# Later places for the prompt-attention and gated-attention pieces among the stretches of the cached attention

## The chip, the cores and the metric

The kernel runs on one core of one Trainium2 chip. The metric is the device time of one execution in microseconds (us). Engines are named as in the profile: PE (TensorE matmul), PEld (its weight load), DVE (VectorE), ACT (ScalarE), POOL (GpSimd) and SP (SyncE, which issues nearly all transfers here).

## What is computed

One decoder layer runs for a prompt group (256 rows) and a sample group (8 sequences of 8 new rows). Between two feed-forward sublayers stands the mixer, whose two head groups share one projection:

```python
qm, km, vm, qg, kg, vg, gg, log_a = mixer_projections(h, pos, w_mix_in, w_gk_up, b_gk)
o_moba = moba_fn(qm, km, vm)          # prompt: causal softmax; sample: top-3 of 8 cached blocks + own rows
o_gla, s_fin = gla_chunked(qg, kg, vg, log_a, gla_s0, gla_chunk)
o_gla = gla_output(o_gla, gg, gla_norm_g, x.dtype)
mix = jnp.concatenate([o_moba, o_gla], axis=-1) @ w_mix_out
x = post_norm_residual(x, mix, m[:, 5], 1.0, ln_g[1], ln_b[1])
```

For the samples `moba_fn` reads a paged cache of 2048 past keys and values per sequence, 8 heads of 64 (`cache_k`, `cache_v`, 256 pages of 256 KB in all). For the prompt it is a plain causal attention over 256 rows. `gla_chunked` is the gated linear attention with a carried state per head.

## The kernel before

The program is written out by hand, engine by engine: each engine has its own list of steps in program order, and semaphores order the lists against each other. The change lies in the stage after the mixer's projections, from about 420 to 630 us of the profile, in which three things are woven together.

**The cached attention.** The 8 sequences go in 4 pairs, i = 0 to 3. A pair's 16 pages of keys per sequence come in four stretches j = 0 to 3 (512 keys of each sequence). A stretch is: PE turns 8 key pages (`turn_keys`, L1046, four 128x128 transposes a page into one PSUM bank); ACT and DVE copy each bank into `kT` (L1445 and L2090, shared between them by `on_act`); PE multiplies with the queries (`scores`, L1057); DVE takes the block sums and block maxima from the scores (`block_values`, L2097 and L2099), and only then ACT copies the scores into `prob` (`scores_out`). After a pair's fourth stretch comes its opening of the softmax: DVE picks the blocks (`choose`, ten small steps L2117 to L2128), ACT takes nine exponentials (`exps`), PE turns the probabilities (`turn_probs`, L1077 and L1079, five banks), DVE copies banks 0, 1 and 4 and ACT banks 2 and 3 into `PT` (`probs_dve`, L2146; `probs_act`), and PE multiplies with the value pages (`values`, L1095) group by group. `own_heads` (DVE L2154), `pick_heads` (PE L1110), `out_high` (ACT) and `out_low` (DVE L2160) carry the result of a pair out. The stretches of pair i+1 run between the value groups of pair i.

**The transfers.** A group is 4 pages, 1 MB. SP issues the 64 groups in the order of `PAGE_GROUPS`; each waits until the group that last held its buffer has been used. There are four ring buffers and one in `pages_h`/`pages_l`; a sixth (`IN_M`, inside the projections `M`) and a seventh (`IN_W`, inside `W`) join later, at the groups that `BEGIN_AT` names, once the projections and the turned prompt values that lie there are no longer needed.

**The pieces.** The prompt's attention and the gated attention are cut into pieces k = 0 to 19 (`mix(k)`, one function on PE, ACT and DVE each). Pieces 0 to 6 are the prompt's attention, two heads at a time and pipelined: scores on PE (L1119, L1120), mask and maximum on DVE (`prompt_max`, L2169 to L2174), exponentials on ACT, normalising on DVE (`prompt_norm`, L2179 to L2182), transposes on PE (L1126), copies on ACT, values on PE (L1135 to L1137), rounding on ACT and DVE (L2186). Pieces 12 to 19 are the gated attention's output and states: 13 and 14 the outputs (L1173 to L1181), 16 a logarithm and an exponential on ACT over 128x1280, 16 to 19 the sample states (PE L1218, DVE L2270 and L2261, two sequences a piece), 17 the scaled output on DVE (L2317), 18 its high half on ACT, 19 its low half on DVE (L2320). Nothing is left in pieces 7 to 11 here: they ran during the projections.

`point(x)` is a place in the weave; `AT_POINT` maps it to a piece. Place 0 to 2 lie in the stretches j = 1 to 3 of pair 0; for pair i the places from 4i+3 on are: 4i+3 first after the scores of its fourth stretch, 4i+4 after the value groups of the second sequence of pair i-1, 4i+5 and 4i+6 in the first two stretches j that follow. (For pair 0, place 3 lies in the first and 4 in the second stretch of pair 1, 5 and 6 in the third and fourth.)

**PSUM.** Every turned page, score, probability or piece takes one of five banks in rotation. PE may fill a bank once ACT or DVE has copied out what was filled five places earlier (`turn_bank`), so a late copy of either engine stops PE.

After the last key stretch PE also starts the output projection: `early_slot(0)` (L836 to L841) waits for `go_done`, the end of piece 19 on DVE; `early_slot(1)` follows among the last value groups.

Of the kernel before, what the change touches and what calls it, by code (L numbers as in the profile page):

```python
# [183 lines left out]
GAPS[10] += [("nvg", t) for t in range(3)]  # L184
FILLS = [key for gap in GAPS for key in gap]
IN_MI = len(FILLS)
AT_POINT = {0: 0, 1: 1, 2: 2} | {x: x - 1 for x in range(4, 8)} | {x: x + 4 for x in range(8, 14)} | {15: 18, 16: 19}


def point_fills(x):  # L190
# [6 lines left out]
for _i in range(NPAIR):  # L197
    _m = 4 * _i + 3
    if _i == 0:
        PAGE_GROUPS += [("k", 1, j, bi) for j in range(2) for bi in range(2)]  # L200
        PAGE_GROUPS += [("v", 0, 0, 0)] + [("k", 1, 2, bi) for bi in range(2)] + [("v", 0, 1, 0)]
        PAGE_GROUPS += [("k", 1, 3, bi) for bi in range(2)] + [("v", 0, 2, 0), ("v", 0, 3, 0)]
        FILLS += key_fills(1, 0) + point_fills(_m) + key_fills(1, 1) + point_fills(_m + 1)
        FILLS += [("p", 0, q) for q in range(5)] + key_fills(1, 2) + point_fills(_m + 2) + [("own", 1)]
        FILLS += key_fills(1, 3) + point_fills(_m + 3)
        continue
    FILLS += point_fills(_m) + point_fills(_m + 1)
    if _i:
        PAGE_GROUPS += [("v", _i - 1, g, 1) for g in range(4)]
        FILLS += [("pick", _i - 1)]  # L210
    FILLS += [("p", _i, q) for q in range(5)]
    for _j in range(4):
        if _i + 1 < NPAIR:
            PAGE_GROUPS += [("k", _i + 1, _j, bi) for bi in range(2)]
            FILLS += ([("own", _i + 1)] if _j == 3 else []) + key_fills(_i + 1, _j)
            FILLS += point_fills(_m + 2 + _j) if _j < 2 else []
        PAGE_GROUPS += [("v", _i, _j, 0)]
PAGE_GROUPS += [("v", NPAIR - 1, g, 1) for g in range(4)]
FILLS += [("pick", NPAIR - 1)]
GROUP_AT = {key: n for n, key in enumerate(PAGE_GROUPS)}  # L220
FILL_AT = {key: n for n, key in enumerate(FILLS)}
IN_RING, IN_H, IN_M, IN_W = range(GROUPS), GROUPS, GROUPS + 1, GROUPS + 2
BEGIN_AT = {GROUP_AT[("v", 1, 1, 0)]: IN_M, GROUP_AT[("v", 2, 0, 0)]: IN_W}
LAST_IN = {IN_H: GROUP_AT[("v", 2, 3, 0)], IN_M: GROUP_AT[("k", 3, 3, 1)], IN_W: GROUP_AT[("v", 3, 0, 0)]}


# [123 lines left out]
def layer_kernel(nc, a, o):  # L350
    ctx = ExitStack()
    with ctx:
# [250 lines left out]
        def _(sp):  # L603
# [73 lines left out]
            def load_pages(n):  # L677

                kind, i, g, bi = PAGE_GROUPS[n]
                cache = a["cache_k"] if kind == "k" else a["cache_v"]  # L680
                _, page = nc.values_load_multi_w_load_instructions(
                    pages[0:1, bass.ds((2 * i + bi) * NPAGE + 4 * g, 4)], engines=[mybir.EngineType.SP],
                    min_val=0, max_val=NPHYS - 1,
                    skip_runtime_bounds_check_because="a page table holds numbers of physical pages")
                b = BUF[n]
                if GROUP_BEFORE[n] is not None:
                    wait_used(GROUP_BEFORE[n])
                elif b == IN_H:
                    sp.wait_ge(used, MI + 12)
                elif b == IN_M:  # L690
                    sp.wait_ge(tp_filled, FILL_AT[("po", 3)] + 1)
                elif b == IN_W:
                    sp.wait_ge(stored, 4 * 16)
                    sp.wait_ge(tp_filled, FILL_AT[("go", 3)] + 1)
                else:
                    sp.wait_ge(lo_ready, split_through(MI + 8 + (b - RING_AT[MI]) % R))
                for j in range(4):
                    sp.dma_start(page_at(b, j), cache[bass.ds(page[j], 1), :, :].rearrange("o s f -> s (o f)")
                                 ).then_inc(page_landed[b], 16)
# [67 lines left out]
        def _(pe):  # L767
# [570 lines left out]
            for i in range(NPAIR):  # L1338
                m0 = 4 * i + 3
                if i == 0:  # L1340
                    turn_keys(1, 0, 0)
                    turn_keys(1, 0, 1)
                    point(m0)
                    scores(1, 0)
                    turn_keys(1, 1, 0)
                    turn_keys(1, 1, 1)
                    point(m0 + 1)
                    scores(1, 1)
                    turn_probs(0)
                    values(0, 0, 0)  # L1350
                    turn_keys(1, 2, 0)
                    turn_keys(1, 2, 1)
                    values(0, 0, 1)
                    point(m0 + 2)
                    scores(1, 2)
                    own_scores(1)
                    turn_keys(1, 3, 0)
                    turn_keys(1, 3, 1)
                    values(0, 0, 2)
                    values(0, 0, 3)  # L1360
                    point(m0 + 3)
                    scores(1, 3)
                    continue
# [8 lines left out]
                for j in range(4):  # L1372
                    if i + 1 < NPAIR:
                        if j == 3:
                            own_scores(i + 1)
                        turn_keys(i + 1, j, 0)
                        turn_keys(i + 1, j, 1)
                    if i == NPAIR - 1 and j == EARLY_SLOT[0]:
                        pe.wait_ge(go_done, 1)
                        wait_dve(("po", HP - 1))  # L1380
                        early_slot(0)
                    values(i, 0, j)
                    if i + 1 < NPAIR:
                        if j < 2:
                            point(m0 + 2 + j)
                        scores(i + 1, j)
            for g in range(4):
                if g == EARLY_SLOT[1]:
# [52 lines left out]
        def _(act):  # L1441
# [296 lines left out]
            for i in range(NPAIR):  # L1738
                m0 = 4 * i + 3
                if i == 0:  # L1740
# [4 lines left out]
                    keys_act(1, 1, 0)  # L1745
                    keys_act(1, 1, 1)
                    exps(0, 6, 9)
                    point(m0 + 1)
                    probs_act(0)
                    scores_out(1, 0)  # L1750
                    scores_out(1, 1)
                    keys_act(1, 2, 0)
                    keys_act(1, 2, 1)
                    point(m0 + 2)
# [12 lines left out]
                if i + 1 < NPAIR:  # L1767
                    for j in range(4):
                        keys_act(i + 1, j, 0)
                        keys_act(i + 1, j, 1)  # L1770
                        if j < 2:
                            point(m0 + 2 + j)
                        scores_out(i + 1, j)
            act.wait_ge(s_out, 8 * NPAIR)
            high(At(MO))
            high(At(MO + 1))
# [36 lines left out]
        def _(dve):  # L1813
# [591 lines left out]
            for i in range(NPAIR):  # L2405
                m0 = 4 * i + 3
                block_values(i, 3)
                if i == 0:
                    keys_dve(1, 0, 0)
                    keys_dve(1, 0, 1)  # L2410
                    choose(0)
                    point(m0)
                    keys_dve(1, 1, 0)
                    keys_dve(1, 1, 1)
                    block_values(1, 0)
                    point(m0 + 1)
                    block_values(1, 1)
                    probs_dve(0, 0)
                    probs_dve(0, 1)
                    totals(0)  # L2420
                    probs_dve(0, 4)
                    keys_dve(1, 2, 0)
                    keys_dve(1, 2, 1)
                    point(m0 + 2)
# [17 lines left out]
                if i + 1 < NPAIR:  # L2442
                    for j in range(4):
# [5 lines left out]
                            point(m0 + 2 + j)  # L2449
                        if j < 3:  # L2450
                            block_values(i + 1, j)
            low(At(MO))
            low(At(MO + 1))
            own_heads(NPAIR - 1)
            out_low(NPAIR - 1)
# [176 lines left out]
```

## Time and profile before

| | us |
|---|---|
| median of 3 runs | 912.74 |
| lowest and highest | 911.48, 916.84 |
| the profiled execution, own time | 915.75 |
| its span, first to last instruction | 914.0 |
| PE busy | 861.1 (94%) |
| DVE busy | 552.1 (60%) |
| ACT busy | 349.0 (38%) |
| HBM read | 196.04 MB |

PE is busy nearly all the time; the stage of the cached attention is where it is not: there its idle time is 22.33 us of 205 (425 to 630 us). A busy PE is also not a PE at full clock: the profile lists the granted clock by slices, and in this stage it falls below 1.00 in several.

### The profile page before, as it was taken

To read this page: it belongs to the slowest core of one execution; us is meant where nothing else is said; L and a number is where in the kernel's file an instruction comes from. 1 tells how busy PE (TensorE), PEld (TensorE's weight loads), DVE (VectorE), ACT (ScalarE), POOL (GpSimd) and SP (SyncE) were. 2 spreads that over 40 slices of the span, in tenths; PEclk is the share of its full clock that TensorE was granted. 3 is DMA by queue.
4 is the path that set the end of the run, shared out by engine and by line. 5 is a ranking of instruction groups with operands and counts; after the bars stand their busy time and mean duration, and the time that the engine had idled before them with its cause. 6 is when DMAs were issued, how large, how long until landed. Compare 5 with 4: busy or idle time off the path is not lost. (4 is left out here: it accounts for less than half of the span.)

```text
span 914.0 us, 17041 instructions
## 1 busy us (share of the span) xinstructions
PE 861.1 (94%) x6857; PEld 758.8 (83%) x6857; DVE 552.1 (60%) x873; ACT 349.0 (38%) x494; POOL 27.8 (3%) x32
## 2 busy tenths in 40 slices
PE   5899999999999999999888998989999999999994
PEld 2588888889999599997566876678799999999993
DVE  1545445545665798785775466662886765555556
ACT  2423222323433654544655335441343322333331
POOL 0000000000000000000000000000300000000002
PEclk9999999999999999999999899999999999999997
DMA  9999898888756544456869989997836555534521
GB/s 318 349 287 276 245 271 254 249 240 226 236 147 216 184 140 151 155 166 218 292 191 362 386 308 386 346 377 239 228 86 171 159 139 143 144 103 128 159 64 57
DMA packets 209028, 200.96 MB, mean 220 GB/s; under 512 B 9601, under 2 KB 161293, under 8 KB 208822
## 3 DMA queue, kind: packets, MB, share of 16 engines
q1 hardware_dynamic: 207556, 196.04, 68.8%
q0 software_dynamic: 704, 2.49, 0.7%
q10 hardware_dynamic: 690, 1.35, 0.5%
q8 instruction: 54, 0.88, 0.4%
q14 instruction: 24, 0.20, 0.1%
HBM read 196.04 MB, written 3.80 MB: 219 GB/s over the span
## 5 line engine op out<-in xcount | busy, mean ns | idle before, releaser
L1826 DVE TENSOR_TENSOR wl<-raw,wh 128x2048 fp32r<-128x2048 f32 x90 | 206.7, 2298 | 90.5 <-ACT wh L1445 90.1
L780 PE MATMUL B<-Hh,wh 128*128 128x320 f32 x864 | 258.9, 313 | 0.4 <-ACT wh L1445 0.3
L781 PE MATMUL B<-Hl,wh 128*128 128x320 f32 x864 | 255.0, 309 | 0.0
L1445 ACT ACTIVATE wh<-raw 128x2048 fp32r<-128x2048 f32 x90 | 172.2, 1913 | 139.4 <-PE B L785 93.3
L780 PEld LDWEIGHTS B<-Hh,wh 128*128 128x128 f32 x864 | 162.1, 188 | 17.3 <-issue 16.2
L781 PEld LDWEIGHTS B<-Hl,wh 128*128 128x128 f32 x864 | 162.3, 188 | 0.3
L785 PE MATMUL B<-Hh,wl 128*128 128x320 f32 x864 | 144.2, 309 | 0.0
L785 PEld LDWEIGHTS B<-Hh,wl 128*128 128x128 f32 x864 | 131.1, 188 | 0.0
L780 PE MATMUL B<-Gh,wh 128*128 128x320 f32 x352 | 104.4, 311 | 0.0
L781 PE MATMUL B<-Gl,wh 128*128 128x320 f32 x352 | 103.8, 309 | 0.0
L1445 ACT ACTIVATE sg<-B 128x320 f32<-128x320 f32 x46 | 20.1, 437 | 194.0 <-PE B L785 179.7
L2007 DVE TENSOR_TENSOR hf<-sg,B 128x320 f32<-128x320 f32 x44 | 21.4, 487 | 100.3 <-ACT sg L1445 100.3
L780 PEld LDWEIGHTS B<-Gh,wh 128*128 128x128 f32 x352 | 66.1, 188 | 0.8 <-issue 0.8
L781 PEld LDWEIGHTS B<-Gl,wh 128*128 128x128 f32 x352 | 66.1, 188 | 0.0
L785 PE MATMUL B<-Gh,wl 128*128 128x320 f32 x352 | 56.8, 309 | 0.0
L1046 PE MATMUL B<-cst,ring 128*128 128x128 f32 x368 | 48.5, 286 | 6.4 <-ACT kT L1445 3.4
L1046 PEld LDWEIGHTS B<-cst,ring 128*128 128x128 f32 x368 | 42.3, 146 | 14.2 <-issue 6.7
L785 PEld LDWEIGHTS B<-Gh,wl 128*128 128x128 f32 x352 | 52.9, 188 | 0.0
L2090 DVE COPY kT<-B 128x512 f32<-128x512 f32 x62 | 41.2, 686 | 16.2 <-PE B L1046 16.1
L1445 ACT ACTIVATE kT<-B 128x512 f32<-128x512 f32 x66 | 36.0, 606 | 13.5 <-PE B L1046 13.5
L882 PE MATMUL B<-raw,cpk 128*32 128x512 f32 x272 | 37.4, 634 | 2.8 <-DMA raw<-in_w_ada 2.5
L1095 PE MATMUL B<-ring,PT 128*32 128x128 f32 x800 | 26.2, 280 | 8.7 <-DMA ring<-in_cache_v 4.6
(286 smaller groups left out, 935.9 us busy)
## 6 DMA issues: line engine op xcount, KB each, us to landing
raw<-in_w_ffn_in SPq DMA_DIRECT2D x88, 512.0 KB, 6.5
raw<-in_w_ada SPq DMA_DIRECT2D x68, 512.0 KB, 4.9
ring<-in_cache_v SPq DMA_DIRECT2D x100, 256.0 KB, 5.1
ring<-in_cache_k SPq DMA_DIRECT2D x92, 256.0 KB, 5.0
raw<-in_w_ffn_out SPq DMA_DIRECT2D x32, 384.0 KB, 3.7
raw<-in_w_mix_in SPq DMA_DIRECT2D x24, 512.0 KB, 4.7
raw<-in_w_ffn_out SPq DMA_DIRECT2D x32, 320.0 KB, 4.3
pages_h<-in_cache_k SPq DMA_DIRECT2D x14, 256.0 KB, 4.1
```

The costliest lines, as they stand in the source:

```text
L780: pe.matmul(out, w, xh[k], start=start and k == 0, stop=False)
L781: pe.matmul(out, w, xl[k], start=False, stop=False)
L785: m = pe.matmul(out, w, xh[k], start=False, stop=stop and k == last)
L882: m = pe.matmul(B[ada_bank(unit)][32 * x:32 * x + 32, :], cpk[:, k, :], v[:, x, :], start=(at == 0), stop=(at == slots - 1))
L1046: m = pe.transpose(bank[:, c * P:(c + 1) * P], at[p][:, c * P:(c + 1) * P], ident)
L1095: m = pe.matmul(out[32 * c:32 * c + 32, :], PT[:, 4 * g + p, 32 * c:32 * c + 32], at[p][:, c * P:(c + 1) * P], start=(g == 0 and p == 0), ...
L1445: return act.activation(out, in_, func, **kw)
L1826: dve.tensor_tensor(dst, raw_view(n), f32(wh[:, wbuf(n), :]), ALU.subtract).then_inc(lo_ready, 1)
L2007: step(dve.tensor_tensor(hf[:, j, :], sg[:, j, :], B[2 * j][:, 0:N], ALU.mult))
L2090: dve.tensor_copy(kT[:, bi, :, p * P:(p + 1) * P], tb(key).rearrange("p (c s) -> p c s", c=HP)).then_inc(tp_dve, 1)
```

## The change

The change gives the pieces later places. `AT_POINT` mapped 0-2 to 0-2, 4-7 to 3-6, 8-13 to 12-17, 15 to 18 and 16 to 19; now it maps 4-10 to 0-6 and 11-18 to 12-19. So pieces 0 to 2 leave pair 0's own stretches, and no piece stands ahead of the first pair's turned probabilities any more; the last two stand between value groups of pair 3, where places 17 and 18 are new. For pair 0, place 4 goes behind `turn_probs(0)` on PE, behind `scores_out(1, 1)` on ACT and behind the last copy of the probabilities on DVE, and `choose(0)` goes ahead of the key copies of pair 1's first stretch. The sixth buffer is freed by piece 3 (the last reader of the prompt's queries and keys) where it waited for piece 6; the seventh joins at group ("v", 2, 2, 0), two value groups later. A wait for `go_done` is added ahead of the second early weight's low half on DVE, whose place in memory piece 19 still reads.

```diff
-AT_POINT = {0: 0, 1: 1, 2: 2} | {x: x - 1 for x in range(4, 8)} | {x: x + 4 for x in range(8, 14)} | {15: 18, 16: 19}
+AT_POINT = {x: x - 4 for x in range(4, 11)} | {x: x + 1 for x in range(11, 19)}
...
-BEGIN_AT = {GROUP_AT[("v", 1, 1, 0)]: IN_M, GROUP_AT[("v", 2, 0, 0)]: IN_W}
+BEGIN_AT = {GROUP_AT[("v", 1, 1, 0)]: IN_M, GROUP_AT[("v", 2, 2, 0)]: IN_W}
...
-                    sp.wait_ge(tp_filled, FILL_AT[("po", 3)] + 1)
+                    sp.wait_ge(tp_filled, FILL_AT[("ps", 7)] + 1)
...
-                    point(m0 + 1)
                     scores(1, 1)
                     turn_probs(0)
+                    point(m0 + 1)
                     values(0, 0, 0)
...
                     values(i, 0, j)
+                    if j < 2:
+                        point(m0 + 2 + j)
                     if i + 1 < NPAIR:
-                        if j < 2:
-                            point(m0 + 2 + j)
                         scores(i + 1, j)
...
                     exps(0, 6, 9)
-                    point(m0 + 1)
                     probs_act(0)
                     scores_out(1, 0)
                     scores_out(1, 1)
+                    point(m0 + 1)
...
                 if i == 0:
+                    choose(0)
                     keys_dve(1, 0, 0)
                     keys_dve(1, 0, 1)
-                    choose(0)
                     point(m0)
...
                     block_values(1, 0)
-                    point(m0 + 1)
                     block_values(1, 1)
                     probs_dve(0, 0)
                     probs_dve(0, 1)
                     totals(0)
                     probs_dve(0, 4)
+                    point(m0 + 1)
...
             low(At(MO))
+            dve.wait_ge(go_done, 1)
             low(At(MO + 1))
```

On PE, around the first pair's turned probabilities, before (L1126 to L1120 are the last nine matmul rows of piece 3, which follows the keys of stretch (1,1); L1057 scores of stretch (1,1), L1077 and L1079 the probabilities, L1095 the first value group):

```order
L1126 MATMUL B<-cst,Z 128x128 x6
L1119 MATMUL B<-M 128x128
L1120 MATMUL B<-M 128x256
L1119 MATMUL B<-M 128x128
L1120 MATMUL B<-M 128x256
L1057 MATMUL B<-kT,Qz 32x512 x8
L1077 MATMUL B<-cst,prob 128x128 x16
L1079 MATMUL B<-cst,arow 128x128
L1095 MATMUL B<-ring,PT 32x128 x16
```

and with the change (line numbers are one higher):

```order
L1047 MATMUL B<-cst,ring 128x128 x32
L1058 MATMUL B<-kT,Qz 32x512 x8
L1078 MATMUL B<-cst,prob 128x128 x16
L1080 MATMUL B<-cst,arow 128x128
L1120 MATMUL B<-M 128x128
L1121 MATMUL B<-M 128x256
L1120 MATMUL B<-M 128x128
L1121 MATMUL B<-M 128x256
L1096 MATMUL B<-ring,PT 32x128 x16
```

The scores now follow the keys at once, and piece 0 stands between the turned probabilities and the first value group.

On ACT, the opening of pair 3, before (`prob<-B` is the last copy of scores, `Hh<-M` piece 18, `prob,small` the exponentials, `Hh<-B` the high half of pair 2's heads, `PT<-B` the probabilities, `wh<-M` the first early weight):

```order
L1445 ACTIVATE prob<-B 128x512
L1445 ACTIVATE Hh<-M 128x1280
L1445 ACTIVATE prob,small<-prob,small 128x256 x8
L1445 ACTIVATE arow,small<-arow,small 128x64
L1445 ACTIVATE Hh<-B 128x4x16
L1445 ACTIVATE PT<-B 128x512 x2
L1445 ACTIVATE wh<-M 128x2048
```

and with the change:

```order
L1446 ACTIVATE prob<-B 128x512
L1446 ACT_TABLE_LOAD
L1446 ACTIVATE Z<-Z 128x1280
L1446 ACT_TABLE_LOAD
L1446 ACTIVATE Z<-Z 128x1280
L1446 ACTIVATE prob,small<-prob,small 128x256 x8
L1446 ACTIVATE arow,small<-arow,small 128x64
L1446 ACTIVATE Hh<-B 128x4x16
L1446 ACTIVATE PT<-B 128x512 x2
L1446 ACTIVATE Hh<-M 128x1280
L1446 ACTIVATE wh<-M 128x2048
```

Piece 16 with its two table loads stands ahead of pair 3's exponentials; it stood behind pair 2's.

On DVE, from the same opening's out_low to the first early weight, before (`Hl<-M` ends piece 19, `Hl<-B` is out_low, `wl<-M` the low half of the early weight):

```order
L2270 SCALAR_TENSOR_TENSOR W<-W,rstd,B 64x128 x8
L2320 TENSOR_TENSOR Hl<-M,Hh 128x1280
L2160 TENSOR_TENSOR Hl<-B,Hh 128x4x16
L2146 COPY PT<-B 128x512 x2
L2135 TENSOR_REDUCE small<-small 128x1
L2136 RECIPROCAL small<-small 128x1
L2146 COPY arow<-B 128x128
L1826 TENSOR_TENSOR wl<-M,wh 128x2048
```

and with the change:

```order
L2164 TENSOR_TENSOR Hl<-B,Hh 128x4x16
L2150 COPY PT<-B 128x512 x2
L2139 TENSOR_REDUCE small<-small 128x1
L2140 RECIPROCAL small<-small 128x1
L2150 COPY arow<-B 128x128
L2274 SCALAR_TENSOR_TENSOR W<-W,rstd,B 64x128 x4
L2265 TENSOR_SCALAR W<-W,cst 64x256
L2274 SCALAR_TENSOR_TENSOR W<-W,rstd,B 64x128 x4
L2265 TENSOR_SCALAR W<-W,cst 64x256
L2274 SCALAR_TENSOR_TENSOR W<-W,rstd,B 64x128 x8
L2324 TENSOR_TENSOR Hl<-M,Hh 128x1280
L1830 TENSOR_TENSOR wl<-M,wh 128x2048
```

Pieces 18 and 19 now stand between the copies of the probabilities and the early weight.

## Rows read from the trace of the kernel before

**Rows 1.** Busy time by stretch: us of each engine, granted clock, DMA share, GB/s.

```profile
425.00:480.00 55.00, 46.05 (x433) 33.07 (x425) 41.89 (x106) 29.61 (x81) 0.00 (x0) 0.97 0.79 263
...
510.00:530.00 20.00, 19.81 (x241) 15.22 (x240) 8.78 (x15) 6.27 (x13) 0.00 (x0) 1.00 1.04 381
...
sum 205.00, PE 182.67 PEld 142.93 DVE 121.36 ACT 89.68 POOL 1.90; mean PE 30.45 PEld 23.82 DVE 20.23 ACT 14.95 POOL 0.32
```

**Rows 2.** PE in order of time, pair 0: start, us, [idle before, releaser].

```profile
444.07 0.63 PE L1046 MATMUL B<-cst,ring 128*128 128x128 f32 x4 [1.55 <-DVE arow L2106]
...
449.80 1.97 PE L1046 MATMUL B<-cst,ring 128*128 128x128 f32 x16
...
454.44 0.66 PE L1046 MATMUL B<-cst,pages_h 128*128 128x128 f32 x4 [2.24 <-ACT kT L1445]
...
466.93 1.97 PE L1077 MATMUL B<-cst,prob 128*128 128x128 f32 x16 [0.66 <-DVE Hl L2186]
...
472.76 1.08 PE L1095 MATMUL B<-ring,PT 128*32 128x128 f32 x32 [3.71 <-DVE PT L2146]
473.77 3.63 PE L1046 MATMUL B<-cst,ring 128*128 128x128 f32 x16
```

**Rows 3.** DVE in order of time, ahead of pair 0's probabilities.

```profile
466.80 0.55 DVE L2169 TENSOR_TENSOR Z<-B,cst 128x384 f32<-128x384 f32 x1
...
470.73 0.68 DVE L2097 TENSOR_REDUCE small<-B 128x2 f32<-128x512 f32 x1
...
471.93 1.28 DVE L2146 COPY PT<-B 128x512 f32<-128x512 f32 x2
```

**Rows 4.** ACT in order of time, piece 3 before.

```profile
464.31 0.39 ACT L1445 ACTIVATE Z<-Z,psm 128x128 f32<-128x128 f32 x1
...
466.32 0.85 ACT L1445 ACTIVATE Z<-B 128x384 f32<-128x384 f32 x2
```

**Rows 5.** PE in order of time, the openings of pairs 1 and 2.

```profile
499.53 1.08 PE L1095 MATMUL B<-ring,PT 128*32 128x128 f32 x32 [1.56 <-DMA ring<-in_cache_v]
...
501.52 1.09 PE L1110 MATMUL B<-cst,arow 128*128 128x64 f32 x4 [0.70 <-DVE arow L2154]
502.40 3.62 PE L1077 MATMUL B<-cst,prob 128*128 128x128 f32 x16
...
557.72 0.33 PE L1079 MATMUL B<-cst,arow 128*128 128x128 f32 x1 [2.40 <-DVE Hl L2160]
...
573.12 1.53 PE L1046 MATMUL B<-cst,ring 128*128 128x128 f32 x12 [2.14 <-ACT kT L1445]
```

**Rows 6.** Busy time by stretch, as in group 1, behind pair 2's opening.

```profile
560.00:565.00 5.00, 5.00 (x57) 4.63 (x56) 2.61 (x4) 1.79 (x3) 0.00 (x0) 0.74 1.06 389
```

**Rows 7.** ACT in order of time, the opening of pair 2.

```profile
547.62 0.51 ACT L1445 ACTIVATE prob<-prob,small 128x256 f32<-128x256 f32 x1
...
552.01 1.28 ACT L1445 ACT_TABLE_LOAD   x1
553.30 1.27 ACT L1445 ACTIVATE Z<-Z 128x1280 f32<-128x1280 f32 x1
...
557.19 0.22 ACT L1445 ACTIVATE Hh<-B 128x64 fp32r<-128x64 f32 x1
```

**Rows 8.** PE in order of time, from pair 3's last scores on.

```profile
589.26 1.90 PE L1057 MATMUL B<-kT,Qz 128*32 128x512 f32 x16
...
605.52 0.42 PE L836 MATMUL B<-Hh,wh 128*128 128x320 f32 x1
...
614.79 1.08 PE L1095 MATMUL B<-ring,PT 128*32 128x128 f32 x32 [1.60 <-DMA ring<-in_cache_v]
...
617.49 1.94 PE L1095 MATMUL B<-ring,PT 128*32 128x128 f32 x32 [1.40 <-DMA ring<-in_cache_v]
```

**Rows 9.** DVE in order of time, the opening of pair 3.

```profile
594.97 1.24 DVE L2270 SCALAR_TENSOR_TENSOR W<-W,rstd,B 64x128 f32<-64x128 f32 x4
...
601.19 1.49 DVE L2320 TENSOR_TENSOR Hl<-M,Hh 128x1280 fp32r<-128x1280 f32 x1
```

More of the change, by code:

```diff
@@ L202 @@
         PAGE_GROUPS += [("k", 1, 3, bi) for bi in range(2)] + [("v", 0, 2, 0), ("v", 0, 3, 0)]
-        FILLS += key_fills(1, 0) + point_fills(_m) + key_fills(1, 1) + point_fills(_m + 1)
-        FILLS += [("p", 0, q) for q in range(5)] + key_fills(1, 2) + point_fills(_m + 2) + [("own", 1)]
+        FILLS += key_fills(1, 0) + point_fills(_m) + key_fills(1, 1)
+        FILLS += [("p", 0, q) for q in range(5)] + point_fills(_m + 1)
+        FILLS += key_fills(1, 2) + point_fills(_m + 2) + [("own", 1)]
         FILLS += key_fills(1, 3) + point_fills(_m + 3)
@@ L215 @@
             FILLS += ([("own", _i + 1)] if _j == 3 else []) + key_fills(_i + 1, _j)
-            FILLS += point_fills(_m + 2 + _j) if _j < 2 else []
+        FILLS += point_fills(_m + 2 + _j) if _j < 2 else []
         PAGE_GROUPS += [("v", _i, _j, 0)]
@@ L1773, in _ @@
                         scores_out(i + 1, j)
+                else:
+                    point(m0 + 2)
+                    point(m0 + 3)
             act.wait_ge(s_out, 8 * NPAIR)
@@ L2451, in _ @@
                             block_values(i + 1, j)
+                else:
+                    point(m0 + 2)
+                    point(m0 + 3)
             low(At(MO))
+            dve.wait_ge(go_done, 1)
             low(At(MO + 1))
```

## Prediction

> **What bounds the kernel now.** I read first the busy time by stretch, then PE's timeline in the stage of the cached attention, and for each idle row of PE the engine that is named as releaser. PE is the bound: from 425 to 630 us it is busy 182.67 of 205 us, so 22.3 us are idle [rows 1]. Transfers are near their limit but not over it: a full stretch moves 381 GB/s at a DMA share of 1.04, while pair 0's stretch moves 263 GB/s at 0.79 [rows 1]. That is the first thing to see: while pair 0 is under way, SP has nothing to issue into, because PE frees the buffers too slowly. The second is why PE is slow there. It waits for DVE or ACT, 1.55, 2.24, 0.66 and 3.71 us [rows 2], and in each of those moments DVE works on a piece of the prompt's attention that stands ahead of the copies PE needs. Ahead of the 3.71 us DVE is in piece 3 from 466.80 to 470.73, 3.93 us of maxima and normalising, then in two pairs of block reductions, and copies the probabilities only at 471.93 [rows 3]. Third, idle time costs twice: behind the 3.71 us sixteen transposes take 3.63 us where sixteen take 1.97 otherwise [rows 2], and behind a wait for transfers sixteen turned probabilities take 3.62 [rows 5]. The granted clock is below 1.00 in such stretches (0.74 from 560 to 565 us [rows 6]): PE is at the lower of its two levels, 1.2 GHz, for part of them, and it had idled just before.
>
> No work is removed by the change. All instructions stay, so the sum is one of idle time and of slow clock.
>
> **Pair 0.** Up to the first value group the four waits go, 1.55 + 2.24 + 0.66 + 3.71 = 8.2 us: with no piece ahead, DVE goes from its block reductions straight to the probabilities, and piece 0 covers the copy on PE. The slow clock behind the last wait goes too, 3.63 - 1.97 = 1.7 us. Two things come in their place. `choose(0)` now stands ahead of the key copies: choosing ends 594.97 - 591.16 = 3.8 us after the scores in pair 3 [rows 8, 9], where 591.16 is the end of the scores, and a key copy adds 0.7, so the fourth page is ready at 4.5 us, while PE's eight pages take 2 x 1.97 = 3.9 [rows 2]: 0.5 us. Pieces 1 and 2 now load DVE in stretches (1,2) and (1,3). Piece 1 repeats the case of the 1.55 us (DVE's maxima ahead of the block reductions and the own block), between 0 and 1.55; I take 1.0, since only part of its 3.9 us of DVE work is left when PE needs the bank. Piece 2's rest falls into pair 1's opening. Sum: -8.2 - 1.7 + 0.5 + 1.0 = **-8.4 us**.
>
> **The opening of pair 1** gets pieces 3 and 4 where piece 6 stood. The path runs through ACT, counted from the end of the scores: the rest of piece 2 on DVE 1.4 (its 3.93 us begin some 2.5 earlier), one pair of block reductions 1.2 [rows 3], the copy of the scores 0.5, piece 3 on ACT 467.17 - 464.31 = 2.9 [rows 4], nine exponentials 552.01 - 547.62 = 4.4 [rows 7], piece 4 on ACT 3.2 (2.9 and a small exponential), the heads' high and low halves and the first copy 1.1. That is 14.7 us, with hand-overs 15. PE has some 11.5 us of work in it: four value groups of 1.08, the probabilities 2.3, the heads 0.6, pieces 3 and 4 about 4.5. So it idles 3.5 us where it idles 1.56 for a transfer now and 0.70 for the heads [rows 5]. The transfer's wait should go, since pages run further ahead. The slow clock there (3.62 for 1.97) I keep as it is. **+1.3 us**, between -1 and +4.
>
> **The opening of pair 2** loses piece 16. Today its logarithm and exponential hold ACT from 552.01 to 557.19, 5.2 us [rows 7]; the high half of pair 1's heads waits behind them, and PE waits 2.40 us for the bank [rows 5]; the clock then falls to 0.74 for 5 us, (1 - 0.74) x 5 = 1.3 us [rows 6]; and 2.14 us go when piece 17 on DVE holds up the next stretch's copies [rows 5]. In their place stand pieces 13 to 15, with a decay exponential and two squares on ACT between `exps` and the heads: about 1.0 us of waiting for the banks, an estimate. Their DVE parts are short and end before the scores. -2.40 - 1.3 - 2.14 + 1.0 = **-4.8 us**.
>
> **The opening of pair 3 and the end of the stage.** Here the 5.2 us of piece 16 reappear ahead of the exponentials. From the end of the scores: 1.2 + 0.5 + 5.2 + 4.4, then heads and first copy 1.1 and hand-overs: the first value group at about 13 us. Then on DVE the other copies 0.6, piece 18 3.2 (two states of 1.24 [rows 9], each with some 0.35 of masked rows for a later one), piece 19 2.5 + 1.49 [rows 9], and about 1.5 of waiting for PE's fills: the early weight's matmuls start near 22 us. Today they start at 605.52 - 591.16 = 14.4 [rows 8]. PE has 4 us more work in that time (two state pieces more), so its idle time grows by 3.8. The low half of the early weight follows on DVE, but PE has the high half's matmuls to do first, so it is covered. In exchange the value pages get those 8 us: the waits of 1.60 and 1.40 us for transfers go, and the slow value group with them (1.94 for 1.08) [rows 8]. The 3 us of waiting should lower the clock; I take 1.5 us from 0 to 2. +3.8 + 1.5 - 3.0 - 0.9 = **+1.4 us**.
>
> The Trainium skill, page "ScalarE: Activation LUTs", section "What ACT_TABLE_LOAD costs", gives about 1283 ns for the load and about 1380 ns of drain with it, 2.66 us for a switch. The row shows the load at 1.28 us and the next activation 1.29 us after its start [rows 7], with no drain between; the measurement decides. By the page piece 16 would cost 2 x 2.66 + 2.5 = 7.9 us and pair 3's opening 2.7 us more.
>
> **Hand-overs.** Some 15 new waits between engines stand on this path; between a copy's end and PE's next row lie 0.1 to 0.2 us, so +2.0 us, from 1 to 3.
>
> **Buffers.** The sixth is freed at piece 3, ahead of where SP needs it. The seventh waits for the last output of piece 14, in pair 3's first stretch; it is used two stretches later, and at 1.05 MB / 381 GB/s = 2.75 us a group the stream keeps up. I cost it at nothing; the store of the sample states, later by some 8 us, has the early slots and the last value groups as cover.
>
> The sum is -8.4 + 1.3 - 4.8 + 1.4 + 2.0 = **-8.5 us**. The profiled execution's own time is 915.75 (span 914.0), so 907.3, a ratio of 0.991; on the median of 912.74 that is **904 us**. With the bounds of the terms (-4 to -14) the forecast's own range is 899 to 909.
>
> **Rivals.** (1) The clock stays up: if the shorter waits of the openings of pairs 1 and 3 leave it at 2.4 GHz, 1.7 and 1.5 us go, with 2 of hand-overs too high: 897 to 899. For it speaks that 1.55, 2.24 and 2.14 us of waiting were not followed by slow rows; against it that the new waits come several in a row.
> (2) The waits only change place. Six moved pieces (1, 2, 5, 13 to 15) stand ahead of a stretch's block reductions as pieces 2 and 17 do now, which cost 2.24 and 2.14; at 1.4 us each, 8.5 us come back, and the time stays at 912, 909 to 918. For it: PSUM has the same five banks and DVE the same work. Against it: the gated pieces have little DVE work there, and DVE is busy for 41.9 of 55 us in pair 0 but for 8.8 of 20 later [rows 1], so there is room.
> (3) Slower: the clock at the end of the stage. If the waits from the probabilities of pair 3 on keep PE at 1.2 GHz through pieces 18 and 19 and both early slots, some 25 us of matmuls take 1.8 times as long (3.62 against 1.97), +20 us less what waits hide: 922. It decides from about 10 us of slow rows on; less leaves the kernel faster. Against it: early slots are dense matmuls, and slow stretches last under 5 us so far.
>
> **How the numbers follow.** About 1% (9 us) is what a measurement of this kernel can tell from no change. I give the forecast 0.60, rival 1 0.12, rival 2 0.21, rival 3 0.07. Below 903.6 lie a little under half of the forecast and all of rival 1: faster by over 1% 0.40. Slower is rival 3, 0.07; the rest, 0.53, is within 1%. The range 896 to 914 leaves out the slower half of rival 2 and rival 3.
>
> **What would show it.** In the new profile the first value group should start near 460 us instead of 472.76, without a wait; GB/s from 425 to 480 should rise over 300; the last scores should end near 576 instead of 591; the early slot should start some 22 us after them, behind a wait for DVE; and the waits for value pages should be gone. Wrong I would be if waits for `kT` copies of over 1 us stand in most stretches of pairs 1 to 3, if the DMA share reads over 1.0 throughout with PE waiting for pages, or if the lower clock reaches through the early slots.

## The result, and the profile after

| | before | after |
|---|---|---|
| median, 20 runs each | 912.53 us (908.37 to 916.84) | 906.35 us (903.38 to 909.12) |
| ratio, 95% interval | | 0.9932 (0.992 to 0.9944) |
| the profiled execution, own time | 915.75 us | 903.49 us |
| its span, mean granted clock | 914.0 us, 0.985 | 901.7 us, 0.992 |

The change saves 6.2 us, 0.68%; the prediction was 904 with a range of 896 to 914. The two profiled executions are 12.3 us apart, twice the difference of the medians: that of after is among its fastest, that of before among its slowest. So rows tell here where the time lies, and the medians how much it is.

The stage splits at six events that both programs have: PE's first value group, the ends of the scores (1,3), (2,3) and (3,3), the first matmul of the early weight and the choosing of the last heads' rows (`pick_heads`). Busy time by these stretches, of the kernel before (columns as in [rows 1]: length, PE, PEld, DVE, ACT, POOL, granted clock, DMA share, GB/s):

```profile
419.98:472.76 52.78, 43.77 (x378) 30.10 (x379) 38.26 (x99) 30.59 (x82) 0.00 (x0) 1.00 0.82 278
472.76:493.80 21.04, 21.04 (x285) 16.49 (x286) 9.94 (x24) 9.50 (x24) 0.00 (x0) 0.92 0.88 290
493.80:543.80 50.00, 47.21 (x620) 38.17 (x620) 25.93 (x54) 20.05 (x49) 0.00 (x0) 0.93 0.96 349
543.80:591.16 47.36, 42.05 (x530) 32.14 (x530) 29.75 (x68) 22.41 (x47) 0.73 (x1) 0.96 1.03 373
591.16:605.52 14.36, 12.53 (x238) 10.34 (x238) 13.54 (x39) 9.23 (x24) 1.17 (x1) 1.00 1.00 352
605.52:630.24 24.72, 21.03 (x308) 19.50 (x305) 4.06 (x3) 1.91 (x1) 0.00 (x0) 0.93 0.75 273
```

The same view of the kernel after, with three stretches more, of which two answer to [rows 1, 6]:

```profile
419.47:459.38 39.91, 38.74 (x329) 26.22 (x330) 25.86 (x52) 23.48 (x53) 0.00 (x0) 1.00 1.02 360
459.38:479.55 20.17, 18.35 (x272) 13.42 (x272) 14.48 (x39) 9.53 (x28) 0.00 (x0) 1.00 0.91 321
479.55:525.60 46.05, 41.98 (x584) 31.80 (x587) 28.99 (x77) 23.81 (x68) 0.00 (x0) 1.00 1.00 365
525.60:574.71 49.11, 46.10 (x620) 36.14 (x612) 26.74 (x57) 20.33 (x50) 0.72 (x1) 1.00 0.99 359
574.71:597.36 22.65, 17.47 (x255) 12.94 (x254) 20.33 (x60) 15.91 (x29) 1.17 (x1) 1.00 1.04 361
597.36:618.76 21.40, 20.70 (x304) 20.00 (x305) 4.83 (x3) 0.00 (x0) 0.00 (x0) 0.92 0.63 214
...
425.00:460.00 35.00, 33.89 (x309) 23.05 (x309) 26.45 (x54) 19.57 (x45) 0.00 (x0) 1.00 1.04 371
...
425.00:480.00 55.00, 52.07 (x562) 36.31 (x560) 40.75 (x92) 28.99 (x72) 0.00 (x0) 1.00 0.99 353
...
560.00:565.00 5.00, 4.81 (x48) 3.56 (x42) 3.25 (x5) 2.48 (x5) 0.72 (x1) 1.00 1.05 379
```

Length less PE's busy time is idle time, and busy time times (1 - clock) is what the lower clock took (the clock has two places, so each of these is good to about 0.2 us). In us:

| stretch | idle, before | idle, after | lower clock, before | lower clock, after |
|---|---|---|---|---|
| pair 0, to the first value group | 9.0 | 1.2 | 0 | 0 |
| to the end of the scores (1,3) | 0 | 1.8 | 1.7 | 0 |
| opening of pair 1, to the scores (2,3) | 2.8 | 4.1 | 3.3 | 0 |
| opening of pair 2, to the scores (3,3) | 5.3 | 3.0 | 1.7 | 0 |
| opening of pair 3, to the early weight | 1.8 | 5.2 | 0 | 0 |
| to the choosing of the last rows | 3.7 | 0.7 | 1.5 | 1.7 |
| sum | 22.6 | 16.0 | 8.2 | 1.7 |

The rest, work at full clock, is 179.5 and 181.7 us. So the stage is 11.0 us shorter (210.3 to 199.3): 6.7 of idle time, 6.5 of clock, and 2.2 lost to somewhat longer work.

PE in order of time, after (start, us, [idle before, releaser]):

```profile
459.38 1.08 PE L1096 MATMUL B<-ring,PT 128*32 128x128 f32 x32
...
471.51 0.63 PE L1047 MATMUL B<-cst,ring 128*128 128x128 f32 x4 [1.55 <-DVE arow L2110]
...
493.15 1.53 PE L1078 MATMUL B<-cst,prob 128*128 128x128 f32 x12 [1.46 <-DVE Hl L2190]
...
495.28 1.16 PE L1047 MATMUL B<-cst,pages_h 128*128 128x128 f32 x8 [0.36 <-DVE PT L2150]
...
528.31 1.08 PE L1096 MATMUL B<-ring,PT 128*32 128x128 f32 x32 [0.96 <-DMA ring<-in_cache_v]
...
531.00 1.08 PE L1096 MATMUL B<-ring,PT 128*32 128x128 f32 x32 [1.62 <-DMA ring<-in_cache_v]
...
572.81 1.90 PE L1058 MATMUL B<-kT,Qz 128*32 128x512 f32 x16
...
587.81 1.08 PE L1096 MATMUL B<-ring,PT 128*32 128x128 f32 x32 [0.32 <-issue]
...
597.36 0.58 PE L837 MATMUL B<-Hh,wh 128*128 128x320 f32 x1 [2.87 <-DVE Hl L2324]
597.73 0.47 PE L838 MATMUL B<-Hl,wh 128*128 128x320 f32 x1
598.00 0.47 PE L837 MATMUL B<-Hh,wh 128*128 128x320 f32 x1
```

The first value group comes at 459.4 without a wait where it came at 472.8 behind 3.71 us [rows 2]. The waits for value pages at the end [rows 8] are gone; two for value pages stand at pair 2's opening instead. The early weight starts behind 2.87 us of waiting for DVE's `Hl`, the end of piece 19.

DVE and ACT in order of time, after, the opening of pair 3 (the last scores end at 574.7):

```profile
578.25 0.23 DVE L2132 TENSOR_SCALAR small<-small 128x8 f32<-128x8 f32 x1
578.52 1.24 DVE L2274 SCALAR_TENSOR_TENSOR W<-W,rstd,B 64x128 f32<-64x128 f32 x4
...
587.03 1.28 DVE L2150 COPY PT<-B 128x512 f32<-128x512 f32 x2
...
588.49 0.29 DVE L2150 COPY arow<-B 128x128 f32<-128x128 f32 x1
589.98 1.24 DVE L2274 SCALAR_TENSOR_TENSOR W<-W,rstd,B 64x128 f32<-64x128 f32 x4 [1.21 <-PE B L1219]
...
595.81 1.49 DVE L2324 TENSOR_TENSOR Hl<-M,Hh 128x1280 fp32r<-128x1280 f32 x1
```

```profile
576.72 1.28 ACT L1446 ACT_TABLE_LOAD   x1
...
581.77 0.49 ACT L1446 ACTIVATE prob<-prob,small 128x256 f32<-128x256 f32 x1
...
586.14 1.06 ACT L1446 ACTIVATE PT<-B 128x512 f32<-128x512 f32 x2
```

Both engines are full: ACT with piece 16 ahead of the exponentials, and DVE without a gap from 574.8 to 588.8, and then with one of 1.21 us, in which it waits for PE to fill a bank. Which of the two sets the early weight's start can't be read from these rows; the runs below tell.

### The profile page after: what moved, and what is told of

It is laid out like the page before. It is cut to its first block and busy times, and to the rows that moved or that the text cites. A ratio compares the mean times of both kernels' runs of the same rounds, so it can differ in the third digit from the quotient of the medians.

```text
span 901.7 us, 17040 instructions
## 1 busy us (share of the span) xinstructions
PE 856.8 (95%) x6857; PEld 752.7 (83%) x6857; DVE 552.0 (61%) x873; ACT 348.3 (39%) x494; POOL 27.8 (3%) x32
## 5 line engine op out<-in xcount | busy, mean ns | idle before, releaser
L1058 PE MATMUL B<-kT,Qz 128*32 128x512 f32 x256 | 31.3, 598 | 0.7 <-DVE kT L2094 0.5
```

Of the source, the lines that this page charges most:

```text
L1058: m = pe.matmul(B[j % 2][32 * c:32 * c + 32, :], Qz[:, 2 * i + bi, c, :], kT[:, bi, c, :], start=(bi == 0), stop=(bi == 1))
```

## The experiments

The theory after the result: pair 0's stretches gain what they no longer wait for; that keeps the stream of pages full, and so the later openings can gain as well; at the end DVE's chain costs some of it. Rivals: the stream does all of it; the terms simply add up, as in the prediction's sum; ACT's piece 16 sets the end. Edits are to the changed kernel, unless said otherwise. A ratio is against the kernel before, on the same chip. That kernel's median was 911.0 to 912.1 us there, against 912.53 above, so a difference between the medians of two runs can be off by 1.5 us; where the ratios tell another difference, it stands beside.

**Only the gated pieces late.** The prompt's pieces, the orders around the first pair's probabilities and the sixth buffer's wait are as in the kernel before.

```diff
-AT_POINT = {x: x - 4 for x in range(4, 11)} | {x: x + 1 for x in range(11, 19)}
+AT_POINT = {0: 0, 1: 1, 2: 2} | {x: x - 1 for x in range(4, 8)} | {x: x + 1 for x in range(11, 19)}
```

> Only the gated pieces 12 to 19 get their later places; the prompt's pieces 0 to 6 and the first pair's choosing stand as in the kernel before. If the gain is mostly pair 0's, as the prediction's sum has it (-8.4 of -8.5 with pair 1's +1.3), this kernel keeps only the openings of pairs 2 and 3 and half of the hand-overs: -4.8 + 1.4 + 1.0 = -2.4 us, near 910 us, a ratio of 0.997. If the later places only work together with an early stream of pages (rival: from pair 1 on the transfers are at their limit, and a stage that starts late stays late), the openings of pairs 2 and 3 gain nothing and it is 912 to 915. If the gated pieces carry most of the gain, it is under 908.

Measured: 920.41 us, ratio 1.0089 (1.0061 to 1.0118), slower than the kernel before by 8 us. None of the three had that. PE in order of time, three of its ten waits for pages:

```profile
516.98 1.08 PE L1095 MATMUL B<-M,PT 128*32 128x128 f32 x32 [1.41 <-DMA M<-in_cache_v]
...
538.75 1.08 PE L1095 MATMUL B<-ring,PT 128*32 128x128 f32 x32 [1.68 <-DMA ring<-in_cache_v]
541.46 1.93 PE L1095 MATMUL B<-ring,PT 128*32 128x128 f32 x32 [1.63 <-DMA ring<-in_cache_v]
```

Without pieces in them, pair 2's stretches ask for pages faster than they come (from 495.0 to 536.2 us the DMA share is 1.05, at 382 GB/s): the ten waits are 9.9 us where the kernel before has three of 4.6 [rows 5, 8]. Its early weight starts 22.7 us after the last scores, as in the changed kernel, against 14.4 before. The terms don't simply add up as the prediction has them: the prompt's late pieces, with the orders that go with them, are worth 14 us on top of the gated ones, and the gated ones alone cost 8. The fourth case, the prompt's pieces late and the gated ones not, wasn't run; so it isn't shown how much of the 14 us the prompt's pieces would bring alone.

**The same three kernels with shorter pages.** All three with this edit:

```diff
+                part = 256 if kind == "v" and b != IN_W else 512
...
-                    sp.dma_start(page_at(b, j), cache[bass.ds(page[j], 1), :, :].rearrange("o s f -> s (o f)")
+                    sp.dma_start(page_at(b, j)[:, 0:part],
+                                 cache[bass.ds(page[j], 1), :, 0:part].rearrange("o s f -> s (o f)")
```

> The kernel before with half of the bytes of each value page left out (256 of a row's 512 numbers, except in the seventh buffer), so that the attention's output isn't the reference's: it shows what PE, ACT and DVE alone set when the stream of pages is some 15 MB shorter. The kernel before waits for value pages at three places (1.56, 1.60, 1.40 us, with 0.9 of slow rows behind the last): if these go and nothing takes their place, 912 - 5.5 = 906 to 908. If the stream is no limit at all: 912.

> The run with only the gated pieces late, with half of the bytes of each value page left out in the same way. Its trace shows ten waits for pages, 9.9 us, from 500 to 545 us at a DMA share of 1.05, and the clock at 0.52 and 0.80 behind the last of them (some 3.4 us). If the pages made it slower than the kernel before, 10 to 13 us go: 907 to 910. If the later places of the gated pieces also gain what the prediction's sum has for them once no page is late (-4.8 for pair 2's opening, +3.8 and +1.5 for pair 3's, +1.0 hand-overs: about +1.5), it stands 1 to 2 us above the shortened kernel before. If its loss has another cause (clock, waits between engines), it stays above 915.

> The changed kernel with half of the bytes of each value page left out in the same way. Its page waits are 0.96 and 1.62 us, so 906.4 - 2.6 = 903 to 904 by the theory that the changed kernel stays just under the stream's limit. By the prediction's terms without those for pages (-8.4, +2.9, -4.8, +5.3, +2.0) it stands 3 us under the shortened kernel before. If the whole gain of the change came from the earlier stream, it equals the shortened kernel before within 1.5 us.

Measured: 908.64 (0.9972; 0.9953 to 0.9991), 915.28 (1.0036; 1.0016 to 1.0056) and 903.52 (0.9916; 0.9896 to 0.9935). The first and third came close to what was expected, 1 us over and within the range. The second missed by 5 us: only 5.1 of the loss went, and six waits for pages, 5.4 us, were left in its trace. In the traces of the first and third PE waits for no page any more, and the change still gains 5.1 us (3 by the prediction's terms without those for pages); so the rival that the stream does all of it falls. And gated pieces alone still lose 6.6 us, where the same terms have 1.5; the six waits that were left are about the difference, though that they are its cause isn't shown. From the last scores to the choosing of the last rows, the shortened kernel before and then the shortened gated-only one:

```profile
588.63:622.88 34.25, 31.73 (x542) 28.83 (x542) 17.60 (x41) 11.15 (x25) 1.17 (x1) 1.00 0.70 224
```

```profile
585.03:629.00 43.97, 37.87 (x559) 32.90 (x558) 25.18 (x62) 15.80 (x29) 1.18 (x1) 0.96 0.61 186
```

By the same split as above the first has 2.5 us idle and no lower clock, the second 6.1 idle and about 1.6 of lower clock. Of the 9.7 us between them 4.5 is work moved there; 5.2 is the real price of the later pieces at the end of the stage.

**ACT's logarithm and exponential early.**

```diff
-                if k == 16:
-                    act.wait_ge(tp_dve, dve_through(FILL_AT[("gm", GH - 1)]))
-                    step(act_(gv, gv, ACT.Ln))
-                    act_(gv, gv, ACT.Exp, scale=-0.5).then_inc(go_r, 1)
...
+                        if i == NPAIR - 2 and j == 2:
+                            act.wait_ge(tp_dve, dve_through(FILL_AT[("gm", GH - 1)]))
+                            step(act_(gv, gv, ACT.Ln))
+                        if i == NPAIR - 2 and j == 3:
+                            act_(gv, gv, ACT.Exp, scale=-0.5).then_inc(go_r, 1)
                         scores_out(i + 1, j)
```

> The changed kernel with piece 16's logarithm and exponential on ACT (5.2 us with their table loads) moved into ACT's idle time ahead of the copies of scores in pair 3's third and fourth stretches. The prediction's chain for the opening of pair 3 ran through ACT: 5.2 us ahead of the exponentials. If that chain sets the early slot, the exponentials start some 3.2 us earlier (DVE's choosing ends at 578.5, they start at 581.8) and the time falls by about 3 us, to 903. If DVE sets it instead (in the changed kernel's trace DVE has no idle time from the block reductions at 574.8 to the probabilities' copies at 588.5), the early slot stays where it is and the time is within 1 us of 906.4.

Measured: 906.37 us, 0.9939 (0.992 to 0.9957), no difference. Its last scores end at 580.2. ACT and PE in order of time:

```profile
584.00 0.51 ACT L1446 ACTIVATE prob<-prob,small 128x256 f32<-128x256 f32 x1 [1.82 <-DVE small L2133]
```

```profile
602.85 0.63 PE L837 MATMUL B<-Hh,wh 128*128 128x320 f32 x1 [2.87 <-DVE Hl L2325]
```

The exponentials start 3.8 us after the scores instead of 7.1, and the early weight 22.65 us after them, as before to a hundredth, behind the same 2.87 us. ACT is off the path; DVE's chain sets it, with its wait of 1.21 us for PE's fill in it as before.

**The low half ahead of the last four states.**

```diff
-                if 16 <= k <= 19:
+                if 16 <= k <= 17:
                     for b in (2 * (k - 16), 2 * (k - 16) + 1):
...
-                    point(m0 + 2)
                     point(m0 + 3)
+                    own_rows(NB - 2)
+                    own_rows(NB - 1)
             low(At(MO))
-            dve.wait_ge(go_done, 1)
+            for b in range(NB - 4, NB):
+                state_new(b)
+            dve.wait_ge(tp_dve, dve_through(FILL_AT[("ss", NB - 1)]))
             low(At(MO + 1))
```

PE waits for the last state ahead of `early_slot(1)`.

> The changed kernel with piece 19's low half on DVE ahead of the last four sample states, which come behind the first early weight's low half. DVE then has 4 states of 1.24 us less, some 5 us, ahead of the early slot. If DVE's chain sets the end of the stage, the early slot starts near 592 to 593 instead of 597.4, PE's idle time of 2.9 us and the slow rows behind it go, and the time falls by 4 to 6 us, to 901 or 902. If the value pages set it (the DMA share is 1.05 up to 600 us), the waits for pages of the kernel before come back, 1.60 and 1.40 us and the slow group behind them, and 1 to 2 us are left of it. If ACT's chain sets it: no change.

Measured: 899.61 us, 0.987 (0.9851 to 0.9888): 6.7 us under the changed kernel (5.7 by the two ratios). PE in order of time:

```profile
593.82 0.42 PE L837 MATMUL B<-Hh,wh 128*128 128x320 f32 x1
594.07 0.31 PE L838 MATMUL B<-Hl,wh 128*128 128x320 f32 x1
...
612.49 1.08 PE L1096 MATMUL B<-ring,PT 128*32 128x128 f32 x32 [0.58 <-DMA ring<-in_cache_v]
```

The early weight starts 19.0 us after the last scores (574.9), without a wait and at full clock, and of the page waits 0.58 us comes back. Expected were 17.3 to 18.3 us, 1 us too few, and a time of 901 or 902 us, 1 to 2 too many.

**Fillers ahead of the early weight.**

```diff
+                        keep_busy(B[MO_BANKS[0]], 14)
                         pe.wait_ge(go_done, 1)
                         wait_dve(("po", HP - 1))
                         early_slot(0)
```

> The changed kernel with five matmuls of 128x512 that nobody reads (0.53 us each by the same line's rows elsewhere) put into the 2.9 us in which PE waits ahead of the early slot (the number of them in the file is five). If the lower clock behind that wait comes from the idle time, the early slot's first rows run at full clock (0.15 us apart for 320 columns where they are 0.27 apart) and 1.5 us are saved; the fillers themselves may delay the slot by up to 0.3. If the clock falls there for another reason, the rows stay slow and the time rises by 0 to 0.3 us.

The text above is wrong about the file: it had fourteen fillers, not five, and one takes 0.88 us, not 0.53 (a matmul here is two rows). They took 12.28 us, and the time was 912.69 (1.0011; 0.9999 to 1.0022). With three:

> The changed kernel with three matmuls of 128x512 ahead of the early slot (fourteen took 12.28 us in the earlier run, 0.88 us each, so three fill 2.6 of the 2.9 us in which PE waits). If the lower clock behind that wait comes from the idle time, the first rows of the early slot run 0.15 us apart and 1.3 to 1.6 us are saved: 905. If not, 906 to 907.

Measured: 903.85 us, 0.9916 (0.9902 to 0.9931). PE in order of time:

```profile
594.07 2.84 PE L910 MATMUL B<-cst 128*128 128x512 f32 x6
597.01 0.41 PE L837 MATMUL B<-Hh,wh 128*128 128x320 f32 x1
597.26 0.31 PE L838 MATMUL B<-Hl,wh 128*128 128x320 f32 x1
597.41 0.31 PE L837 MATMUL B<-Hh,wh 128*128 128x320 f32 x1
```

In the changed kernel the rows behind the wait lie 0.27 us apart until 600.9, here 0.15 from the start; from the early weight to the last rows' choosing it takes 19.9 us for 21.4. So the wait costs its 2.87 us and another 1.5 in lower clock behind it. By the medians it is 2.5 us and by the ratios 1.5, with intervals that just overlap.

**Pieces 0 to 2 back in pair 0.**

```diff
-AT_POINT = {x: x - 4 for x in range(4, 11)} | {x: x + 1 for x in range(11, 19)}
+AT_POINT = {x: x for x in range(3)} | {x: x - 4 for x in range(7, 11)} | {x: x + 1 for x in range(11, 19)}
```

> The changed kernel with only pieces 0 to 2 back in the first pair's own stretches (places 0 to 2; pieces 3 to 6 and 12 to 19 stay late, and no piece stands ahead of the first pair's turned probabilities). By the prediction's working the waits of 1.55 and 2.24 us of the kernel before come back there, while the wait of 1.55 us in stretch (1,2) and DVE's normalising ahead of pair 1's block reductions (1.4 us) go: +1 to +2 us, 907 to 908.5. If it is the early stream of pages that carries the gain (GB/s from 425 to 460 falls back from 350 to some 300), pages are late in the stretches after it and it is 910 or more. If the four waits do not add up at all, it is within 1 us of 906.4.

Measured: 910.85 us, 0.9992 (0.997 to 1.0014): 4.5 us of the gain (5.5 by the ratios) hang on these three pieces. PE in order of time, and one stretch:

```profile
446.46 0.63 PE L1047 MATMUL B<-cst,ring 128*128 128x128 f32 x4 [1.55 <-DVE arow L2110]
...
456.83 0.66 PE L1047 MATMUL B<-cst,pages_h 128*128 128x128 f32 x4 [2.24 <-ACT kT L1446]
...
483.15 0.77 PE L1096 MATMUL B<-pages_h,PT 128*32 128x128 f32 x16 [2.15 <-DMA pages_l<-in_cache_v]
```

```profile
425.00:460.00 35.00, 29.89 (x260) 19.76 (x262) 27.39 (x72) 19.14 (x48) 0.00 (x0) 1.00 0.93 311
```

The two waits of [rows 2] are back as they were, and beyond them come 2.15 and 0.53 us for pages: 311 GB/s where the changed kernel has 371 leaves the first pairs' value pages late. Both parts of the theory are seen in it, and the prediction's way of counting (1 to 2 us) has only the first.

**Choosing behind the key copies.** `choose(0)` back behind `keys_dve(1, 0, 0)` and `keys_dve(1, 0, 1)`.

> The changed kernel with the first pair's choosing behind the key copies again, as in the kernel before. The prediction put 0.5 us of waiting on the choosing ahead of them (the trace shows 0.47). Behind them the exponentials start 2 to 3 us later on ACT; if the probabilities have room (the first value group did not wait), the time is 0 to 0.5 us less, so within 1 us of 906.4; if not, a wait of 1 to 2 us appears at the turned probabilities: 907.5 to 908.5.

Measured: 905.65 us, 0.994 (0.9917 to 0.9963), no difference; the first value group comes 40.1 us after the stage's start instead of 39.9. The wait of 0.47 us is gone, and one of 0.38 us for a key copy stands in its place.

**Both ends together**, the low half first and ACT's functions early.

> The low half ahead of the last four states on DVE (which gave 899.6) together with the logarithm and exponential in pair 3's third and fourth stretches on ACT (which alone gave 906.4, the early slot 22.65 us after the last scores as without it). In the trace of the first DVE has no idle time from the block reductions to the low half, so ACT's earlier exponentials should still bring nothing: 899.6, within 1 us. If ACT became the bound once DVE's chain is shorter, 897 to 898.

Measured: 900.06 us, 0.9899 (0.9862 to 0.9935): nothing on top of the low half, also with DVE's chain shorter. The early weight starts 19.0 us after the last scores, as it does with the low half alone.

**Normalising later**, on top of the low half first.

```diff
-                if 1 <= k <= 4:
+                if 2 <= k <= 4:
                     prompt_norm(2 * (k - 1))
...
                     keys_dve(1, 3, 0)
                     keys_dve(1, 3, 1)
+                    prompt_norm(0)
+                    prompt_norm(1)
                     point(m0 + 3)
```

> The low half ahead of the last four states, and DVE's normalising of piece 1 (1.3 us) behind the key copies of stretch (1,3) where it stood ahead of the block reductions of (1,2). The wait of 1.55 us for the own block's bank in that stretch is put down to DVE's maxima and normalising; if so it falls to some 0.2 us and the time to 898.3 (by 1.3 us), unless pages in later stretches are late by as much (the DMA share is 1.05 there), then 899.6.

Measured: 897.54 us, 0.985 (0.9823 to 0.9876), the fastest of all. PE in order of time:

```profile
470.25 0.63 PE L1047 MATMUL B<-cst,ring 128*128 128x128 f32 x4 [0.23 <-DVE arow L2111]
```

The wait fell from 1.55 to 0.23 as expected; the medians' 2.1 us (1.8 by the ratios) against the kernel without it lie within the intervals of both.

## Why the prediction was right, and where not

The time was right: -8.5 us forecast, -6.2 measured, inside the forecast's own 899 to 909. Its terms against the stretches of the two profiled executions, which add up to the stage's 11.0 us:

- **Pair 0, -8.4.** Idle time to the end of the scores (1,3) fell by 6.0 and the lower clock by 1.7: -7.7. The four waits went as worked out, though two rows were misread: behind piece 3 stands one pair of block reductions on DVE, not two, and ahead of the wait of 0.66 us DVE itself waited 2.51 us for ACT's half of the piece. The 0.5 for choosing was a wait of 0.47; run alone it is worth nothing. Piece 1's wait, taken at 1.0 between 0 and 1.55, came as 1.55 whole.
- **Opening of pair 1, +1.3.** Idle time in its stretch rose by 1.3. From the scores' end (479.6) to the next keys (495.3) it took 15.7 us for the 15 of the chain. (PE's work there adds up to 11.7 us in the prediction's own terms, not 11.5, which changes little.) Wrong was the clock, kept as it was: the 3.3 us of lower clock in that stretch went, though the new idle times come several in a row (0.62, 0.73, 0.23, 1.46 and 0.36). So the term came out at -2.0.
- **Opening of pair 2, -4.8.** -4.0: 2.3 of idle time and 1.7 of clock. The ACT and DVE waits went, and the 1.0 us for banks didn't come: up to 553 us PE waits for nothing but value pages, 2.58 us. This is the term that was mis-founded: it took the stream to keep up. The gated-only run shows what it is worth when pages are not early: its idle time there falls by 0.8 us, and the lower clock, read in steps of half a us, rises by 0.7.
- **Opening of pair 3 and end, +1.4.** +0.4 of idle time and 0.2 of clock. Its gross price, 3.8 + 1.5, is confirmed by the pair with shorter pages (5.2), and the early weight started at 22.65 us for the 22 worked out. But the reason given was wrong in part: the 5.2 us of piece 16 on ACT are not on the path, DVE's chain is.
- **Hand-overs, +2.0.** Work at full clock is 2.2 us longer, but a hand-over as the prediction has it, 0.1 to 0.2 us between a copy's end and PE's next row, would be idle time, and that is counted above. So the two numbers agree by luck, and what made the work longer isn't shown.
- **Buffers, nothing.** No wait names them, but the step as a whole, that terms of different places can be summed with the stream at no cost, is the one that failed. By the sum the gated pieces alone should gain 2.4 us; they lose 8.

So the mechanism was right where it counted most, in pair 0, and that the total came out within 2.3 us is in part luck: pair 1's clock gave 3.3 us that the sum didn't have, pair 2's gain needed early pages that it took for granted, and the profiled pair's 11.0 us in the stage stand against 6.2 us by the medians.

**The rivals.** That waits only change place (909 to 918) didn't come: 22.6 us of idle time became 16.0. The slow end (922) didn't either: the lower clock ended at 600.9. The clock stayed up at pair 1's opening, half of the first rival, and the time is still above its 897 to 899.

**What stays open.** The profiled pair differs by 12.3 us and the medians by 6.2. 6.5 of the 11.0 us in the stage are lower clock, and over the 20 runs of the changed kernel the time goes with the mean clock, from 903.4 us at 0.992 to 909.1 at 0.984; so part of the profiled difference is most likely chance in how often the clock fell. Which falls of the clock the median run has isn't shown: there is one profiled execution of each kernel. For the same reason the gated-only kernel's 8 us are told by the medians; its own profiled execution was only 2.2 us longer than that of before.

## What to carry to other kernels

When several engines and a stream of transfers are all near their limit, a move is not worth the waits that it removes, but what is late next: ask of each stretch both which engine and whether its pages would then come in time, and test halves of the move alone. Work off the bounding engine belongs where that engine has slack and the stream is full; here that was the prompt's pieces out of the stage's start, while the gated pieces at its end cost 5 us until DVE did first what the next weight waits for. Of two engines that are both full ahead of a wait, only a run that relieves one of them tells which sets it.

## What the hardware showed unexpectedly

A fall of the clock in this stage cost 1.5 to 1.7 us in four of the five stretches above that have one, and 3.3 us, twice that, in the fifth (before, 493.8 to 543.8; there the granted clock is 0.50 from 502.4 to 508.0 us, so the prediction's "slow stretches last under 5 us so far" misread it). The changed kernel's fall behind 2.87 us of waiting cost no more than those behind shorter waits. All seven traces with this wait show it: in the 3 us behind it the granted clock is 0.50 to 0.55. A shorter wait doesn't always bring a fall. Ahead of the same twelve transposes the kernel before and the gated-only one both wait 1.55 and 1.54 us for DVE, then 0.27 for ACT. PE in order of time, of the kernel before and then of the gated-only run:

```profile
444.97 1.53 PE L1046 MATMUL B<-cst,ring 128*128 128x128 f32 x12 [0.27 <-ACT kT L1445]
```

```profile
444.55 2.80 PE L1046 MATMUL B<-cst,ring 128*128 128x128 f32 x12 [0.27 <-ACT kT L1445]
```

1.53 us in one execution and 2.80 in the other. Of the thirteen traces here with this pair of waits nine show 1.53 us and four 2.04 to 2.82. The wait of 2.14 us that the prediction's first rival counts among those without slow rows [rows 5] has them in the kernel before with shorter pages:

```profile
568.98 2.82 PE L1048 MATMUL B<-cst,ring 128*128 128x128 f32 x12 [2.14 <-ACT kT L1447]
```

A prediction can therefore put a chance on a fall behind a wait of this size, but not a sum.
